# Q, K and V projections of a forgetting-attention kernel, done in column chunks over two PSUM banks beside the head pairs

## What is computed

```python
def shared_kv(x, p):
    h = rmsnorm(x, p["norm_kv_g"])
    proj = jnp.einsum("btd,de->bte", h, p["w_kv"])
    ...
    logf = jax.nn.log_sigmoid(proj[..., 2 * hd:].astype(jnp.float32) + p["b_forget"].astype(jnp.float32))

def fox_attention(x, p, j, k, v, fk, fq, kpos, qpos):
    h = rmsnorm(x, p["norm_b_g"][j])
    q = jnp.einsum("btd,de->bte", h, p["w_q"][j]).reshape(bsz, t, N_HEADS, HEAD_DIM)
    ...
        s = jnp.einsum("bqhd,bkhd->bhqk", q_blk, k, preferred_element_type=jnp.float32) * scale
        s = s + fq_blk[..., :, None] - fk_t[:, :, None, :]
        s = jnp.where(mask, s, -jnp.inf)
        pr = jax.nn.softmax(s, axis=-1)
        return jnp.einsum("bhqk,bkhd->bqhd", pr.astype(v.dtype), v)
```

## Time and profile before

| | |
|---|---|
| median of three runs | 2831.93 us |
| the profiled execution | 2829.43 us |
| its span | 2827.6 us |
| PE busy | 2733.9 us, 97% |
| DVE busy | 1393.3 us, 49% |
| ACT busy | 833.0 us, 29% |
| mean granted TensorE clock | 0.988 |

### The profile page before, as it was taken

The page is one execution under the profiler, slowest core; times in us unless marked ns, Lnnn a source line. Parts: engine busy times, 40 slices in busy tenths (PEclk is TensorE's granted clock), DMA queues, the critical chain, the costliest instruction groups (busy, mean ns, idle before and its releaser), DMA issues.

```text
span 2827.6 us, 40913 instructions
## 1 busy us (share of the span) xinstructions
PE 2733.9 (97%) x16951; PEld 2656.2 (94%) x16951; DVE 1393.3 (49%) x1905; ACT 833.0 (29%) x1270; POOL 119.4 (4%) x82
## 2 busy tenths in 40 slices
PE   8999999999999999999989999889999999999998
PEld 8999999999999999988888888779999999999998
DVE  6876354244244244455667556564542442442444
ACT  6765321111111112333444344452210110211121
POOL 1000100000000000300000000002000000000000
PEclk9999999999999999999999999899999999999999
DMA  3112111111111111133222232211111111111112
GB/s 131 42 45 99 41 53 37 55 46 42 50 45 42 50 45 43 51 106 94 77 76 75 84 98 84 68 45 46 45 39 53 46 39 54 45 44 49 45 44 79
DMA packets 91331, 166.32 MB, mean 59 GB/s; under 512 B 18066, under 2 KB 55154, under 8 KB 91026
## 3 DMA queue, kind: packets, MB, share of 16 engines
q1 hardware_dynamic: 91154, 163.72, 19.0%
HBM read 141.60 MB, written 13.70 MB: 55 GB/s over the span
## 4 chain that ended last, share of the span: by engine, by line
PE 86%; DVE 6%; ACT 3%; issue 3%; DMA 1%; DVEq 0%; SPq 0%; ACTq 0%
PE psum L368 77%; DVE SB L1656 2%; PE psum L1211 2%; PE psum L1179 1%; PE psum L1193 1%; PE psum L1152 1%; ACT SB L906 1%; PE psum L1134 1%; DVE PTL L1674 1%; DMA NF<-nf_scratch 1%; ACT PTH L921 1%; DVE SB L1666 1%; DVE X L1634 1%; DVE WL L359 0%; DVE X L1777 0%
## 5 line engine op out<-in xcount | busy, mean ns | idle before, releaser
L368 PE MATMUL psum<-XH,WH 128*128 128x352 f32 x2904 | 641.6, 329 | 12.4 <-DVE KS L471 6.3
L368 PE MATMUL psum<-XL,WH 128*128 128x352 f32 x2904 | 626.9, 324 | 0.0
L368 PE MATMUL psum<-XH,WL 128*128 128x352 f32 x2904 | 626.7, 323 | 0.0
L350 ACT ACTIVATE WH<-WR 128x1024 fp32r<-128x1024 f32 (+2 forms) x217 | 215.3, 992 | 1032.3 <-PE psum L368 1020.7
L368 PEld LDWEIGHTS psum<-XH,WH 128*128 128x128 f32 x2904 | 489.2, 189 | 16.1 <-issue 14.5
L368 PEld LDWEIGHTS psum<-XH,WL 128*128 128x128 f32 x2904 | 497.2, 187 | 1.6
L368 PEld LDWEIGHTS psum<-XL,WH 128*128 128x128 f32 x2904 | 493.5, 188 | 1.6
L1529 DVE TENSOR_TENSOR X<-psum,X 128x1056 f32<-128x1056 f32 x63 | 79.2, 1258 | 371.1 <-PE psum L368 371.1
L359 DVE TENSOR_TENSOR WL<-WR,WH 128x1024 fp32r<-128x1024 f32 (+2 forms) x217 | 246.0, 1134 | 9.0 <-ACT WH L350 8.9
L368 PE MATMUL psum<-FYH,WH 128*128 128x352 f32 x1134 | 245.3, 324 | 0.0
L368 PE MATMUL psum<-FYH,WL 128*128 128x352 f32 x1134 | 244.4, 323 | 0.0
(11 more groups left out here) (238 smaller groups left out, 3173.3 us busy)
## 6 DMA issues: line engine op xcount, KB each, us to landing
WR<-in_wfi SPq DMA_DIRECT2D x96, 512.0 KB, 3.5
WR<-in_wfo SPq DMA_DIRECT2D x64, 384.0 KB, 3.1
WR<-in_wa SPq DMA_DIRECT2D x24, 512.0 KB, 3.6
WR<-in_wqkv SPq DMA_DIRECT2D x24, 512.0 KB, 4.6
X<-in_xT SPq DMA_DIRECT2D x16, 528.0 KB, 5.6
CC<-in_ck SPq DMA_DIRECT2D x128, 64.0 KB, 1.8
CC<-in_cv SPq DMA_DIRECT2D x128, 64.0 KB, 2.0
NF<-nf_scratch SPq DMA_DIRECT2D x15, 512.0 KB, 4.9
```

The source lines that it names most:

```text
L350: nc.scalar.activation(WH[:, par, 0:n], WR[:, par, 0:n], ACT.Copy).then_inc(w_hi, 1)
L368: mm = nc.tensor.matmul(psum[0:m, 3 * slot + c, 0:CH], w, x[:, k, c * CH:(c + 1) * CH], start=(k == 0 and part == 0), stop=(k == nk - 1 an ...
```

## The change

The projections of the next pair are done in nine chunks of 352 columns (`CHUNKS`: Q and K by columns 0, 1, 2, V by 2, 1, 0), each with all its eight k-steps in a row, in banks 3 and 4 by turns. `STEPS` places 72 steps of three matmuls among the units where `KSTEPS` placed 24 of nine. A chunk may start when the chunk two before it has been evicted (`bank_free`), and DVE evicts chunk by chunk (`chunk_in`): Q's at v = 3, 5 and 8, K's at v = 9, 12 and 13, V's at v = 16 and twice at the start of the next pair. Bank 5, which this frees, takes every other output (`O_odd`), so that two doubles of output stand in two banks. The high splits of weights move from v = 1, 7, 14 to 3, 7, 13, the low splits from 2, 8, 15 (ahead of the normalisation) to 4, 7, 14 (behind it); the odd head's key halves move from v = 3 to 4 on ACT and 5 on DVE. The odd head's gate row gets a place of its own, the weight buffer that is free from the low split at v = 7 on, and the next pair's even row is loaded behind `maximum(8)`. In the last pair SB gets a third home, in a weight buffer (`sb`), `maximum(v)` waits for `turn(v - 3)`, the load of the second output weight waits for `turn(14)`, and the low split of output tile 1 moves behind the last addition. Left out of the diff are the new semaphores' names and places where `SB[:, v % 2]` became `sb(c, v)`.

```diff
@@ -72,10 +72,12 @@
-SPLIT_SLOTS = [1, 7, 14]
+HI_SLOTS = [3, 7, 13]
+LO_SLOTS = [4, 7, 14]
...
-KSTEPS = [2, 1, 1, 1, 2, 1] + [1] * 6 + [2, 1, 1, 1, 1, 2, 2]
+STEPS = [4, 3, 2, 4, 5, 4, 3, 4, 3, 4, 3, 5, 4, 4, 3, 4, 3, 5, 5]
+CHUNKS = [(r, ch) for r in range(3) for ch in ((2, 1, 0) if r == 2 else (0, 1, 2))]
@@ -232,7 +234,9 @@
         O_ps = psum[:, 2, :]
+        A_ps = [psum[:, 3, 0:CH], psum[:, 4, 0:CH]]
         T_alt = psum[:, 3:5, :].rearrange("p a b -> p (a b)")
+        O_odd = psum[:, 5, :]
         T_ps = psum[:, 6:8, :].rearrange("p a b -> p (a b)")
@@ -253,7 +257,19 @@
         def o_double(d):
-            return O_ps[:, 2 * P * (d % 2):2 * P * (d % 2 + 1)]
+            return (O_ps if d % 2 else O_odd)[:, 0:2 * P]
+
+        def sb(c, v):
+            if c < NHP - 1:
+                return SB[:, v % 2, :]
+            return (SB[:, 0, :], SB[:, 1, :], WR[:, (J_O + 1) % 2, :])[v % 3]
+
+        def bias_of(c, v):
+            if v == 0:
+                return DM
+            if v <= NQB:
+                return NF
+            return NF_last if c == NHP - 1 else WR[:, (J_QKV + 3 * c + 5) % 2, :]
@@ -576,7 +593,8 @@
                 wait(sp, s_read, u0)
-                sp.dma_start(NF[:, :], ins["nf"][2 * hp, :].partition_broadcast(P)).then_inc(nf_ld, 16)
+                if c == 0:
+                    sp.dma_start(NF[:, :], ins["nf"][0, :].partition_broadcast(P)).then_inc(nf_ld, 16)
                 if not last:
@@ -591,9 +609,12 @@
                     sp.wait_ge(k_out, 16 * NHP)
                 else:
+                    sp.wait_ge(w_ready, J_QKV + 3 * c + 6 + 6 * t)
+                sp.dma_start(bias_of(c, 1 + NQB)[:, 0:SEQ],
+                             ins["nf"][2 * hp + 1, :].partition_broadcast(P)).then_inc(nf_odd, 16)
+                if not last:
                     sp.wait_ge(s_read, u0 + 1 + NQB)
-                sp.dma_start((NF_last if last else NF)[:, :],
-                             ins["nf"][2 * hp + 1, :].partition_broadcast(P)).then_inc(nf_ld, 16)
+                    sp.dma_start(NF[:, :], ins["nf"][2 * hp + 2, :].partition_broadcast(P)).then_inc(nf_ld, 16)
                 if c == NHP - 2:
                     load_weights(sp, ins["wo"][0], J_O)
@@ -604,6 +625,7 @@
             over_pairs(sp, pair)
+            sp.wait_ge(t_done, UNITS * NHP - 2)
             for d in range(1, KT):
@@ -894,7 +916,7 @@
                         queries_hi(c, t, 1)
-                    if v == 3:
+                    if v == (3 if c == NHP - 1 else 4):
                         keys_hi(c, t, 1)
@@ -932,8 +954,8 @@
                                              ACT.Copy).then_inc(o_half, 1)
-                    if v in SPLIT_SLOTS and c < NHP - 1:
-                        hi_weights(act, *jq(4 + SPLIT_SLOTS.index(v)))
+                    if v in HI_SLOTS and c < NHP - 1:
+                        hi_weights(act, *jq(4 + HI_SLOTS.index(v)))
                     if c == NHP - 1 and v == UNITS - 1:
@@ -1093,20 +1115,34 @@
             def pair(c, t):
                 u0, last = UNITS * c + 2 * UNITS * t, c == NHP - 1
-                steps = [] if last else [(r, k) for r in range(3) for k in range(KT)]
+                steps = [] if last else [(n, k) for n in range(len(CHUNKS)) for k in range(KT)]
+
+                def bank_free(n):
+
+                    if n < 2:
+                        pe.wait_ge(acc_read, J_QKV + 3 * (c + 1) + 6 * t)
+                    elif n % 3 == 1:
+                        pe.wait_ge(acc_read, J_QKV + 3 * (c + 1) + n // 3 + 6 * t)
+                    else:
+                        pe.wait_ge(qkv_rd, 6 * c + 2 * ((n - 2) // 3) + (n - 2) % 3 + 1 + 12 * t)
                 def project():
-                    if not steps:
-                        return
-                    r, k = steps.pop(0)
+                    n, k = steps.pop(0)
+                    r, ch = CHUNKS[n]
                     first = J_QKV + 3 * (c + 1) + r
+                    if n % 3 == 0 and k == 0:
+                        pe.wait_ge(w_ready, first + 1 + 6 * t)
                     if k == 0:
-                        pe.wait_ge(w_ready, first + 1 + 6 * t)
-                        pe.wait_ge(acc_read, first + 6 * t)
-                    mm = k_step(k, 1, first % 2, XH, XL, KT)
+                        bank_free(n)
+                    wh = WH[:, first % 2, k * P:(k + 1) * P]
+                    wl = WL[:, first % 2, k * P:(k + 1) * P]
+                    for w, y, part in ((wh, XH, 0), (wh, XL, 1), (wl, XH, 2)):
+                        mm = nc.tensor.matmul(A_ps[(c + n) % 2], w, y[:, k, ch * CH:(ch + 1) * CH],
+                                              start=(k == 0 and part == 0), stop=(k == KT - 1 and part == 2),
+                                              skip_group_check=True)
                     if k == KT - 1:
-                        mm.then_inc(job_done, 1)
+                        mm.then_inc(job_done if n % 3 == 2 else qkv_mm, 1)
                 def values():
@@ -1201,9 +1237,10 @@
                     h, i = UNIT_OF[v]
                     pe.wait_ge(pt_lo, (UNITS - 1) * c + v + 2 * (UNITS - 1) * t)
-                    if d == 0:
+                    if d == 1:
                         pe.wait_ge(o_half, PVS * c + 1 + 2 * PVS * t)
-                    wait(pe, o_read, NQB * c + d + 2 * NQB * t if c or d else 0)
+                    elif c or d:
+                        pe.wait_ge(o_read, NQB * c + d - 1 + 2 * NQB * t)
                     for kb in range(i + 2):
                         b = 0 if kb <= i else 1
@@ -1229,6 +1266,7 @@
                             pe.wait_ge(acc_read, J_O)
                             pe.wait_ge(pt_lo, (UNITS - 1) * NHP - 1)
+                            pe.wait_ge(o_read, NQB * NHP - 1)
                             o_k_step(0)
                         if v >= 4 and v % 2 == 0:
@@ -1238,7 +1276,7 @@
                         values()
-                    for _ in range(KSTEPS[v]):
+                    for _ in range(STEPS[v]):
                         project()
@@ -1579,12 +1617,25 @@
+            def chunk_in(c, t, n, out):
+
+                r, ch = CHUNKS[n]
+                if n % 3 == 2:
+                    dve.wait_ge(job_done, J_QKV + 3 * (c + 1) + r + 1 + 6 * t)
+                else:
+                    dve.wait_ge(qkv_mm, 6 * c + 2 * r + n % 3 + 1 + 12 * t)
+                cols = slice(ch * CH, (ch + 1) * CH)
+                nc.vector.tensor_tensor(out[:, cols], A_ps[(c + n) % 2], RS[:, cols], ALU.mult
+                                        ).then_inc(acc_read if n % 3 == 2 else qkv_rd, 1)
+
             def v_in(c, t):
-                dve.wait_ge(job_done, J_QKV + 3 * c + 3 + 6 * t)
-                wait(dve, v_t, 2 * c + 4 * t)
-                wait(dve, v_out, 16 * c + 32 * t)
-                scaled(dve, 1, VS[:, :]).then_inc(acc_read, 1)
+                if c == 0:
+                    dve.wait_ge(job_done, J_QKV + 3)
+                    scaled(dve, 1, VS[:, :]).then_inc(acc_read, 1)
+                    return
+                chunk_in(c - 1, t, 7, VS)
+                chunk_in(c - 1, t, 8, VS)
@@ -1646,15 +1697,16 @@
                     rows, n = (2 * NS, DK) if v == 0 else (P, P * (UNIT_OF[v][1] + 1))
-                    bias = DM if v == 0 else NF_last if c == NHP - 1 and v > NQB else NF
-                    wait(dve, t_done, u0 + max(v - 1, 0))
-                    if v in (1, 1 + NQB):
-                        dve.wait_ge(nf_ld, 16 * (2 * c + 1 + (v > 1)) + 64 * t)
+                    wait(dve, t_done, u0 + max(v - 2 if c == NHP - 1 else v - 1, 0))
+                    if v == 1:
+                        dve.wait_ge(nf_ld, 16 * (c + 1) + 32 * t)
+                    if v == 1 + NQB:
+                        dve.wait_ge(nf_odd, 16 * (c + 1) + 32 * t)
                     wait_apart(dve, qk_done, u0 + v + 1, logits_seen)
                     nc.vector.tensor_tensor_reduce(
-                        SB[0:rows, v % 2, 0:n], S_ps[0:rows, 0:n], bias[0:rows, 0:n],
+                        sb(c, v)[0:rows, 0:n], S_ps[0:rows, 0:n], bias_of(c, v)[0:rows, 0:n],
                         -SCALE, 3.0e38, ALU.add, ALU.min, nmax[0:rows, v:v + 1]).then_inc(s_read, 1)
@@ -1673,13 +1725,6 @@
                                             ALU.subtract).then_inc(pt_lo, 1)
-
-                def spread(v):
-
-                    if v == 2:
-                        queries_lo(c, t, 1)
-                    if v == 3:
-                        keys_lo(c, t, 1)
@@ -1689,44 +1734,48 @@
                         if 1 <= v <= UNITS:
                             normalise(v - 1)
+                        if v >= 6 and v % 2 == 0:
+                            add_halves(c, t, (v - 6) // 2)
                         if v == UNITS + 1:
                             o_split_lo(0)
-                        if v == UNITS + 3:
-                            o_split_lo(1)
-                        if v >= 6 and v % 2 == 0:
```

(43 more changed lines are left out.)

7 lines of the change are left out of this document (3 added, 4 removed).

## The result

The changed kernel takes 2864.45 us in the median (2860.31 to 2870.75), beside 2829.81 us for the kernel before in the same comparison: ratio 1.0125, interval 1.0099 to 1.015. It is slower by 35 us, as forecast (2870, range 2824 to 2888). Its profiled execution took 2860.31 us.

A forecast was written before the change was run, and what follows sets the result against it. The prediction took PE, 97% busy, as the bound, losing time inside head pairs to a late, in-order DVE. 2829.4 + 45.5 (seven pairs) - 5 (last pair) = 2869.9, stated as 2870 us, range 2824 to 2888.

The forecast's parts named there:

- The sign: Whole kernel: the change makes it slower, chance 0.71, against faster 0.20 and same 0.09.
- Rival (a): Head pairs: evictions are in time and PE's waits go, so the kernel is faster, 2806 us; chance 0.20.
- The pair: Each of seven head pairs grows: +7.1 us by DVE's order, taken as +6.5 for rounding; +45.5 us in all.
- The five waits: PE waits for late evictions at chunks 2, 3, 4, 6 and 8: 6.6 to 7.0 us a pair.
- Evictions: On DVE, three of 1.26 us become nine of about 0.52 us: +0.9 us a pair.
- Chains in one bank: Projection matmuls, 24 in a row into one bank: cost zero, at most 2 us a pair.
- rival (d): Projections: single-bank chains are slower, +2 us a pair on top, 2885 us; chance 0.02.
- rival (c): Head pairs: added waits lower PE's granted clock, two more us a pair make 24 us, 2894 us; chance 0.06.
- Splits: Low halves of weights on DVE, moved behind the normalisation where nothing hides them: +3.1 us a pair.
- Gate rows: Odd gate row's load: maximum(9) waits about as long as now; 0.2 us of gain allowed, ends 1.2 and 0.
- Output in two banks: Products no longer wait for the previous addition: three stalls a pair become 0.4 us shorter, +1.2 us.
- Last pair: Third buffer frees maximum(v) from turn(v-2), shortening waits for turns: -5 us, range 0 to -7.

The follow-up runs named there:

- x_evict: The changed kernel with each chunk's eviction directly behind maximum(v), ahead of the wait for the exponential: 2829.57 us, ratio 0.9998.
- b_split: The kernel before with only the splits of weights at the changed kernel's places, low halves behind the normalisation: 2851.5 us, ratio 1.008.
- x_split: The changed kernel with the three splits of weights back at their old places, evictions staying late: 2854.75 us, ratio 1.0086.
- b_gate: The kernel before with the changed kernel's gate rows and the middle split one unit earlier: 2822.07 us, ratio 0.9966.
- x_oone: The changed kernel with evictions and low weight splits ahead of the normalisation, and the output in halves of one bank as before: 2825.42 us, ratio 0.9985.
- c_after: The changed kernel, unedited, run once more on the chip of the next three runs: 2869.47 us, ratio 1.014.
- b_home: The kernel before with only the third home of SB in the last pair and the later load of the second output weight: 2824.31 us, ratio 0.9985.
- x_last: The changed kernel with the low splits of output tiles 0 and 1 ahead of the last two additions: 2859.49 us, ratio 1.011.
- x_gate2_last: The changed kernel with evictions and low weight splits ahead of the normalisation, middle split one unit earlier, output-tile low splits ahead of the last additions: 2790.69 us.
- x_both: The changed kernel with evictions ahead of the normalisation and splits of weights back at their old places: 2824.85 us, ratio 0.9983.
- x_gate: The changed kernel with early evictions and old split places, the middle low split one unit earlier but its high half still at v = 7: 2832.97 us.

## Why the prediction was right, point by point

**The sign and its cause.** Right, and shown from both sides: x_evict takes the 35 us away by moving seven evictions of a pair ahead of DVE's waits, b_split makes 22 us by moving three splits the other way. DVE has 49 to 50% of the span busy in all of these; what counts is whether an operation stands ahead of the waits for ACT or behind them. Rival (a) was this same kernel with its evictions in time. Its condition (chunk 0 out within 1.9 us of logits(4)) failed in after, 2.8 us, and holds in x_evict, 0.4. But its price, 2806, did not come there either: x_evict takes 2829.57, with 27.5 us of waits for nmax and PTL left in six pairs.

**The pair, +6.5 us forecast, +4.8 measured: a term mis-sized.** Along the forecast's walk, forecast, then measured in the mean of seven pairs, then in pair 2 alone: ahead of maximum(3) −1.5, −1.0, +0.1; maximum(3) to maximum(9) +4.9, +3.8, +4.2 (22.5 to 26.7 us); from there to the low half of unit 16 +3.7, +3.1, +2.3 (33.4 to 35.6); the end of the pair 0, −1.2, −1.3 (4.0 to 2.7). So the two long stretches were over-sized by 1.7 us together and the end by 1.2. Pair 2, the only one that the forecast walked, is a poor sample of the first stretch. PE has nine matmuls fewer there, but it starts the first of them 5.4 us behind the store where it was 4.6, and the decode product and turn(1) take 5.8 us instead of 5.0: the granted clock is 0.50 from 1416 to 1422, where before had 0.50 from 1413 to 1415 only. The end was left out of the sum: of V only two chunks are still to be evicted between the pairs, and one of them is early. And the waits of PE were not to be added to the old ones ("some 13 a pair"): listed are 48.5 us in six pairs, 8.1 each. While PE waits for a chunk DVE catches up, so nmax fell from 11.7 to 7.9 and X from 10.2 to nothing.

**The five waits.** Forecast 1.2, 1.2, 1.6, 1.1 and 1.5 to 1.9, 6.6 to 7.0 a pair; measured 0.98 in the mean for the three on QS, 0.8 on KS, 1.6 on VS, 5.4 a pair.

**Evictions.** By shape, in six pairs (busy, ns in the middle of three):

```profile
L1628 DVE TENSOR_TENSOR VS<-psum,RS x20: 511/524/526, 1310.9 to 1839.6; 128x352 f32<-128x352 f32 x20
L1628 DVE TENSOR_TENSOR QS<-psum,RS x18: 503/515/516, 1336.3 to 1800.1; 128x352 f32<-128x352 f32 x18
```

0.52 was forecast from the nearest row. An estimate from the Trainium skill ("VectorE: DVE Perf Modes", the section on the TRN2 errata, its table row for VectorE out of PSUM) is 0.49, which the trace doesn't bear out. The forecast's +0.65 by that row also mixed it with the measured 1.26; with 1.225 for the old length it is +0.75. (The view has 20 rows of V, as its window takes in two chunks of the pair before.)

**Chains in one bank.** Inside a chunk matmuls start 0.16 us apart, as 1425.94 and 1426.10 above: no cost, rival (d) didn't come.

**The clock.** 0.97 in the pairs before and after, so rival (c) didn't come. Nor did the swings of the clock come that the Trainium skill ("TensorE: Matmul & The Clock Gate", the section on psum-queue depth-cycling) reports of a kernel that cycles through PSUM banks: two banks by turns left the clock in the pairs at 0.97.

**Splits.** 3.1 forecast, 3.2 in b_split. That it fits so closely is partly luck: the term counted DVE's own time, while in b_split the middle split is paid through the gate row, and the clock over the pairs is 0.96 instead of 0.97, some 6 us (estimate: 0.01 of 601 us). In after itself they weigh less (15 us in x_split), and next to nothing more once evictions are in time and the gate row is late.

**Gate rows.** The forecast said a wait about as long as now and allowed 0.2 us. In after the waits for the row are 5.3 us in six pairs, 1.4 the longest. That the split which releases it can go one unit earlier, and that row and split then give 9.6 us by themselves (b_gate), it did not see.

**Output in two banks.** −1.2 a pair was named in the forecast, though not in its sum; the waits for X went, but no time was shown to follow (x_oone).

**Last pair, −5 forecast, +2.6 measured.** In the trace of c_after it is +6.8, so the size hangs on the clock behind the pair. The third home had the right sign (b_home −4.6 by medians, 2.4 of it seen in the traces). "o_split_lo(1) is 0.4 us later" was the mis-sized term: it counted the addition and not what the addition waits for. It takes 5 to 6 us by the medians (x_last, x_gate2_last), at least what the home gains: 2 us of it are PE's waits, and the rest goes with half clock, which not every trace has. In spans the sum was +40.5: 12.1 too many in the pairs, 7.6 too few here, 4.4 that went ahead of the pairs, and 0.7 elsewhere; +30.9 came. By the medians it is 5.5 us that the forecast was too high, and that is less than either of its two errors, which have opposite signs: the closeness is luck, the sign and the five waits are not.

## What to carry to other kernels

For an engine that is half idle but works in order, ask of each operation whether it stands ahead of a wait (free) or behind it (paid in full by whoever needs what comes next): here 74 us of 2864 were order alone (after against x_gate2_last). Finer chunks and more banks bring nothing until the evictions that free them come in time, and then the next late release, a load bound to a moved step, has to be moved with them. When a step is moved behind another, count what that other one waits for, not its length.

## What the runs showed of the hardware

A wait costs PE more than its listed idle time. In the lines above (chunk 2 of pair 2) the idle time is 0.82 us, but from 1424.53 to 1426.10 three starts take 1.57 us where they otherwise take 0.48: 1.09 lost. Of the 0.27 between the two, 0.16 is that undisturbed matmuls overlap in the listing (0.32 long, 0.16 apart) and the idle time is counted from the listed end; the other 0.11 is that the next start is 0.27 behind the first matmul and not 0.16. In six pairs before has 48 listed waits and after 69, 3.5 more a pair. That makes some 0.9 us (estimate: 3.5 x 0.27) of the 4.8 that the table of waits doesn't show (there the pair grew by 2.2).

Some waits inside the pairs were followed by half clock. 0.50 is 1.2 GHz, 1.00 is 2.4 GHz. In x_both the granted clock fell to 0.50 for some microseconds within 2 us of each of the six long waits for nmax (1.9 to 3.0 us), in b_split of five of six (2.4 to 2.6), in x_oone of five of six (1.75 to 2.4) and in x_gate of four of six (3.2 to 3.3); in after of one of seven (1.6 to 1.8), in x_evict of none of six (1.5 to 1.8) and in before of none of three (1.4 to 2.3). Behind the wait of 2.05 us at 1440.32 in x_both the stretches read:

```profile
1440.00:1442.00 2.00, 1.68 (x7) 1.44 (x8) 1.09 (x5) 1.67 (x4) 0.00 (x0) 0.81 0.41 162
1442.00:1444.00 2.00, 2.00 (x8) 2.00 (x8) 2.00 (x4) 0.33 (x1) 0.84 (x1) 0.50 0.01 2
```

And in before, behind the longest:

```profile
1693.51 0.50 PE L1152 MATMUL psum<-KHH,QHL 128*128 128x512 f32 x1 [2.34 <-DVE nmax L1656]
```

```profile
1694.00:1696.00 2.00, 2.00 (x14) 1.66 (x12) 1.20 (x3) 1.49 (x4) 1.30 (x1) 1.00 0.00 0
```

So the length of the wait alone doesn't decide it. Over 1240 to 1800 the granted clock is 0.95 in x_both, x_gate and x_oone, 0.96 in b_split, and 0.97 in before, after and x_evict. 0.02 of clock over 560 us is 11 us of PE (estimate), which can be why x_both is only 5 us below x_evict although its listed waits are some 8 us shorter. That this half clock comes from those waits is what the lines suggest; no run was made for it alone.
